# A row of gathers moved beside a projection, eight value buffers, dot products written in place

## The chip, the cores and the metric

The kernel runs on one core of a Trainium2 chip. It uses TensorE (PE in the profile), VectorE (DVE), ScalarE (ACT), GpSimd (POOL) and SyncE (SP), and the core's 16 DMA engines. The metric is the device time of one execution in microseconds, lower is better. The kernel before takes 2611.32 us, the median of three runs (2607.83 to 2613.70).

## The reference, cut to what matters

The reference is two blocks of a network on 256 tokens of width 2048. The first block (attention, a spatial gate, a merge, an output projection) and most of the second are dense products; the change doesn't touch them. It touches the end of the second block, the product-key retrieval of experts, with 8 heads, 16 experts each out of 16384, in two chunks of 128 tokens:

```
def chunk(zc):
    q = (zc @ peer_wq).reshape(128, 8, 2, 128)
    s1 = einsum('chd,hkd->chk', q[:, :, 0], k1);  s2 = einsum('chd,hkd->chk', q[:, :, 1], k2)
    v1, i1 = top_k(s1, 16);  v2, i2 = top_k(s2, 16)
    cand = v1[..., :, None] + v2[..., None, :]          # 16 x 16 sums
    top_s, top_pos = top_k(cand, 16)                    # and the expert numbers i1 * 128 + i2
    gate = softmax(top_s)
    act = gelu(einsum('chkd,cd->chk', peer_u[expert], zc))
    return einsum('chk,chkd->cd', gate * act, peer_v[expert])
```

`peer_u` and `peer_v` have 16384 rows of 2048 float32. Every token takes its own 128 experts, so 2 x 256 x 128 rows of 8 KB are read. The result is added to the residual, and a last RMS norm with the gain `norm_f_g` gives the output.

## The kernel before, in words

All products take their weights in panels of 256 output columns. SP loads a panel as two halves of 1 MB into four slots of RAW; ACT copies each quarter of it rounded into WH; DVE writes the remainder into WL (`split_next`, DVE L1017); PE multiplies WH and WL with the activations' two parts XH and XL (96 matmuls a panel, L1621). PE signals `w_used` after each quarter, and only then may ACT and DVE write the quarter of the next panel. PSUM banks 0 and 1 take the panels in turn, and DVE clears them (`bank_free`). WH, WL, XH and XL lie in the region EX.

The query projection is the last section of that kind: "wq", 8 panels, one per head. DVE clears each panel into `qp` (L1508, in RZ), PE makes the head's key scores for both halves of the tokens (`key_scores`, L1908) after the product of the next panel, and ACT clears these into `scores`. PE also turns the residual into token order with an identity matmul (`token_order`, L1893), 32 instructions for each half; ACT and DVE make of it `znat`, the normed tokens, in two halves (`token_norm`).

A "row" is one head of one half of the tokens: 16 rows, r = 0 to 15, with 16 experts k = 0 to 15. `choose` (DVE) finds the experts of a row in 28 short dependent instructions, in 11 pieces; it leaves their numbers in `idxu` and a copy in `idxv`. In the panels' time `choose` of row 0 lies at panels 1 to 4, that of row 1 at panels 5 to 7.

For each expert k of a row, POOL issues an indirect DMA that gathers 128 rows of `peer_u` (1 MB, one row for each token) into one of four buffers in RAW, and DVE multiplies it with `znat` and sums (the dot, L1542); the products go to two scratch buffers in EX. After 16 dots, DVE and ACT make the row's 16 weights (L1546 to L1557); ACT makes a diagonal matrix of each (L990), and PE multiplies it with the gathered 128 rows of `peer_v` (EX, four buffers, 8 matmul records of L1932) and adds into the half's four PSUM banks. POOL's order is: U gathers of row 0; then for each row r and each k, V gather (r, k) and U gather (r+1, k). Each waits for its buffer to be free. In the last row DVE adds up the experts k with k % 4 in (1, 3) itself (L1578, L1580), and half of the V gathers go to the U buffers. The rows run in hardware loops of two rows for most of the way.

POOL is in order: a gather whose buffer isn't free holds all gathers behind it. The same is true of DVE: a dot whose gather has not landed holds every instruction behind it.

Of the kernel before, what the change touches and what calls it, by code (L numbers as in the profile page):

```python
# [106 lines left out]
def vec_columns():  # L107
# [29 lines left out]
    "dve_step", "act_step", "pool_step", "uz_step", "soft_step", "top_step", "gel_step",  # L137
)
AHEAD = 4


def build(nc, T, out):
# [3 lines left out]
    with ctx:  # L146
# [7 lines left out]
        u_free = [ctx.enter_context(nc.semaphore(f"u_free{s}")) for s in range(4)]  # L154
        v_landed = [ctx.enter_context(nc.semaphore(f"v_landed{s}")) for s in range(4)]
        v_free = [ctx.enter_context(nc.semaphore(f"v_free{s}")) for s in range(4)]
        diag_ready = [ctx.enter_context(nc.semaphore(f"diag_ready{s}")) for s in range(4)]
# [82 lines left out]
        junk = [view(EX, 0, D), view(EX, D, D)]  # L240
        gfbc = view(EX, 2 * D, D)
        vacc = junk[0]
        ON_DVE = (1, 3)

        def last_slot(k):

            s, n = k % 4, k // 8
            if k % 8 < 4:
                return vbuf[s], v_landed[s], (ROWS - 1) * 64 + 16 * (n + 1), v_free[s], (ROWS - 1) * 4 + 1 + n
            return ubuf[s], u_landed[s], ROWS * 64 + 16 * (n + 1), u_free[s], ROWS * 4 + 1 + n  # L250

        ubuf = [view(RAW, (s + 2) % 4 * D, D) for s in range(4)]
        vbuf = [view(EX, (4 + s) * D, D) for s in range(4)]
# [12 lines left out]
        dist = sb("dist", [P, 800])  # L266
        cmask = sb("cmask", [P, 32])
        slopes = sb("slopes", [P, HEADS])
        slcur = sb("slcur", [P, REP])
        gates = sb("gates", [P, HEADS, 6])  # L270

        lruC = gates[:].rearrange("p h s -> p (h s)")[:, 0:8 * BT]
        gcur = sb("gcur", [P, REP, 6])
        vecs = sb("vecs", [P, VEC_COLS])
        hid = sb("hid", [P, 2, 2 * NC_BLOCKS])
        kcT = sb("kcT", [P, 2, NCP])
        kcpad = sb("kcpad", [P, 2, GROUPS, NCP])
        qcur = sb("qcur", [P, 2, TOK])
        vcur = sb("vcur", [P, 5, 3 * HD])
        th = sb("th", [P, 2, PANEL * 2])  # L280
        hidt, hidn = (th[0:SPANS, n, 0:2 * P].rearrange("p (s e) -> p s e", s=2) for n in range(2))
        gin = sb("gin", [P, PANEL * 2])
# [98 lines left out]
        def _(sp):  # L381
# [69 lines left out]
            sp.wait_ge(S["w_used"], QUARTERS * PANELS)  # L451
# [9 lines left out]
        def _(g):  # L461
# [133 lines left out]
            for s in range(4):  # L595
                g.sem_inc(u_free[s], 1)
                g.sem_inc(v_free[s], 1)
# [45 lines left out]
        def _(a):  # L643
# [311 lines left out]
            for j in range(8):  # L955
                if j < 7:
                    split_next("wq", j)
# [1024 lines left out]
```

## Time and profile before

| | |
|---|---|
| median of three runs | 2611.32 us |
| profiled execution | 2612.46 us, its span 2610.7 us |
| PE, busy share | 2204.6 us, 84% |
| DVE | 1523.4 us, 58% |
| POOL | 704.8 us, 27% |
| gathers | 539 MB in 512 gathers |
| DMA rate by fortieths of the span, 1 to 20 | 114 to 261 GB/s |
| 22 to 39 | 403 to 422 GB/s |

The program has two parts. For the first 1300 us PE is busy and the DMA engines are about half busy. From about 1340 us to the end the DMA engines are busy all the time, and PE waits for them. A duration in a row is that of one instruction; behind "idle before" stands for how long the engine did nothing before it, and who ended that. For a POOL gather the duration is that of its issue, not of its transfer.

### The profile page before, as it was taken

How to read it: one execution, taken by the hardware profiler on the slowest of the kernel's cores; microseconds unless marked ns; L12 is line 12 of the kernel's file. 1: busy time of each engine (PE TensorE's matmuls, PEld its weight loads, DVE VectorE, ACT ScalarE, POOL GpSimd, SP SyncE). 2: the span in 40 equal slices, each digit the busy share in tenths (PEclk: the TensorE clock that was granted, in tenths of full speed). 3: DMA queues.
4: the chain of work that ended last, by engine and by line, in shares of the span. 5: the costliest groups of instructions: out<-in, count | busy, mean ns of one | idle time of the engine just before them, and what ended most of it. 6: DMA issues, size and time to landing. Idle time of an engine off the chain costs nothing.

```text
span 2610.7 us, 32711 instructions
## 1 busy us (share of the span) xinstructions
PE 2204.6 (84%) x12156; PEld 1609.4 (62%) x12156; DVE 1523.4 (58%) x2128; ACT 691.4 (26%) x1139; POOL 704.8 (27%) x657
## 2 busy tenths in 40 slices
PE   7999999999999999899937777777777777777776
PEld 7999999999999989899912222222223222332232
DVE  4445655555556587846675565556655556655544
ACT  5434544444344345435300000000000001000001
POOL 3000000000001443020073444434444444444342
PEclk9999999999999999999969999999999999999999
DMA  9634444455657544464499999999999999999997
GB/s 261 193 114 146 138 151 131 137 183 166 222 169 238 162 143 157 135 216 157 146 365 421 421 422 421 421 419 409 403 414 404 422 422 422 418 422 422 421 421 309
DMA packets 280706, 754.64 MB, mean 289 GB/s; under 512 B 11969, under 2 KB 213153, under 8 KB 213793
## 3 DMA queue, kind: packets, MB, share of 16 engines
q0 software_dynamic: 74432, 539.07, 50.3%
q1 hardware_dynamic: 205936, 214.23, 26.2%
q8 instruction: 58, 0.95, 0.2%
q14 instruction: 40, 0.32, 0.0%
q10 hardware_dynamic: 240, 0.07, 0.0%
HBM read 751.22 MB, written 2.10 MB: 289 GB/s over the span
## 4 chain that ended last, share of the span: by engine, by line
PE 55%; DMA 38%; DVE 3%; issue 3%; ACT 1%; POOL 0%; POOLq 0%; DVEq 0%; SPq 0%; ACTq 0%
PE PS L1621 40%; DMA EX<-in_peer_v,idxv 34%; PE PS L1932 9%; DMA RAW<-in_peer_u,idxu 2%; DMA RAW<-in_peer_v,idxv 1%; PE PS L1756 1%; DVE WL L1017 1%; PE PS L1676 1%; PE PS L1734 1%; DVE XL L1027 0%; PE PS L1744 0%; PE PS L1856 0%; POOL RAW L604 0%; PE PS L1758 0%; DMA RZ<-in_x 0%
## 5 line engine op out<-in xcount | busy, mean ns | idle before, releaser
L1932 PE MATMUL PS<-EX,RK 128*128 128x512 f32 x1952 | 914.6, 614 | 355.9 <-DMA EX<-in_peer_v,idxv 273.1
L1932 PEld LDWEIGHTS PS<-EX,RK 128*128 128x128 f32 x1952 | 359.6, 194 | 910.3 <-issue 813.9
L1542 DVE CUSTOM_DVE_ANT_0 EX<-RAW,RZ 128x2048 f32<-128x2048 f32 x256 | 586.8, 2293 | 479.0 <-DMA RAW<-in_peer_u,idxu 435.6
L1621 PE MATMUL PS<-XH,WH 128*128 128x256 f32 x3024 | 839.2, 286 | 11.7 <-DVE WL L1017 8.1
L1621 PE MATMUL PS<-XH,WL 128*128 128x256 f32 x3024 | 832.6, 284 | 0.0
L1621 PE MATMUL PS<-XL,WH 128*128 128x256 f32 x3024 | 761.8, 284 | 5.1 <-DVE XL L1027 3.1
L1017 DVE TENSOR_TENSOR WL<-RAW,WH 128x1024 fp32r<-128x1024 f32 x380 | 480.0, 1274 | 412.1 <-ACT WH L658 409.6
L1621 PEld LDWEIGHTS PS<-XH,WH 128*128 128x128 f32 x3024 | 582.0, 192 | 15.8 <-issue 9.7
L1621 PEld LDWEIGHTS PS<-XH,WL 128*128 128x128 f32 x3024 | 582.2, 193 | 0.0
L658 ACT ACTIVATE WH<-RAW 128x1024 fp32r<-128x1024 f32 x380 | 400.1, 1058 | 566.4 <-PE PS L1621 564.8
L1621 PEld LDWEIGHTS PS<-XL,WH 128*128 128x128 f32 x3024 | 539.9, 193 | 5.9 <-DVE XL L1027 3.5
L604 POOL DMA_INDIRECT EX<-in_peer_v,idxv x240 | 268.5, 1119 | 600.6 <-PE PS L1932 572.8
L604 POOL DMA_INDIRECT RAW<-in_peer_u,idxu x256 | 274.1, 1071 | 201.4 <-DVE WL L1017 90.1
L990 ACT ACTIVATE RK<-identh,wk 128x128 f32<-128x128 f32 x248 | 94.5, 398 | 826.1 <-PE PS L1932 819.5
L518 POOL TENSOR_SCALAR_AFFINE_SELECT RG<-RG 128x1024 f32<-128x1024 f32 x1 | 1.1, 1088 | 514.5 <-ACT RG L791 514.5
L979 ACT ACTIVATE ath<-ain 128x16 f32<-128x16 f32 x16 | 3.5, 216 | 358.4 <-DVE ain L1548 358.4
L524 POOL TENSOR_TENSOR RK<-RZ 128x512 f32 x16 | 17.1, 1068 | 215.6 <-DVE RZ L1283 148.8
L540 POOL MEMSET RK<- 128x1024 f32 x1 | 1.0, 962 | 181.3 <-PE PS L1828 181.3
L768 ACT ACTIVATE RG<-RG,nmx 128x256 f32<-128x256 f32 (+2 forms) x96 | 37.7, 394 | 45.6 <-DVE nmx L1170 45.6
L577 POOL TENSOR_TENSOR RZ<-RZ 128x540 f32<-128x540 f32 (+3 forms) x10 | 15.1, 1508 | 55.3 <-DVE RZ L1315 54.8
L525 POOL TENSOR_TENSOR RK<-RK 128x512 f32<-128x512 f32 x16 | 26.8, 1675 | 1.3
L1174 DVE RECIPROCAL fac<-sums 128x6 f32<-128x6 f32 x16 | 3.1, 192 | 40.3 <-ACT RG L768 40.3
(326 smaller groups left out, 1183.0 us busy)
## 6 DMA issues: line engine op xcount, KB each, us to landing
RAW<-in_w_in SPq DMA_DIRECT2D x110, 1024.0 KB, 5.2
RAW<-in_w_out SPq DMA_DIRECT2D x32, 1024.0 KB, 5.4
RAW<-in_w_ple_gate SPq DMA_DIRECT2D x16, 1024.0 KB, 5.4
RAW<-in_peer_wq SPq DMA_DIRECT2D x16, 1024.0 KB, 5.5
RAW<-in_w_up_a SPq DMA_DIRECT2D x8, 1024.0 KB, 5.4
RAW<-in_w_up_b SPq DMA_DIRECT2D x8, 1024.0 KB, 5.4
RAW<-in_peer_u,idxu POOLq DMA_INDIRECT x256, 16.4
EX<-in_peer_v,idxv POOLq DMA_INDIRECT x248, 15.3
```

What stands on the lines that cost most here:

```text
L525: step(g.tensor_tensor(acc[:, 0], acc[:, 0], sqt[:, 0], ALU.add))
L604: g.indirect_dma_start(buf[s], None, table, bass.IndirectOffsetOnAxis(ap=idx[:, par, k:k + 1], axis=0)).then_inc(landed[s], 16)
L658: a.activation(WH[:, q], raw[:, slot, at:at + QUARTER_KT, :], ACT.Copy).then_inc(S["wh_ready"], 1)
L768: ins = a.activation(eT[:, at:at + size], sT[:, at:at + size], ACT.Exp, bias=nmx[:, n:n + 1], accum_out=sums[:, n:n + 1])
L990: a.activation(diag[:, s, :], identh[:], ACT.Copy, scale=wk[:, par, k:k + 1]).then_inc(diag_ready[s], 1)
L1017: v.tensor_tensor(WL[:, q], raw[:, slot, at:at + QUARTER_KT, :], WH[:, q].bitcast(f32), ALU.subtract).then_inc(S["wl_ready"], 1)
L1542: v.tensor_tensor_reduce(out=junk[k % 2], in0=ubuf[s], in1=znat[:, hf, :], scale=1.0, scalar=0.0, op0=ALU.mult, op1=ALU.add, accum_out=act ...
L1621: ins = mm(o[:, t, :], w[:, q, k, c], x[:, n, :], start=(begins and k == t == m == 0), stop=(ends and k == QUARTER_KT - 1 and m == len(pai ...
L1676: ins = mm(bank(2 + s)[0:SPANS, 0:P], blocks, w1bd[:, s, l, :], start=(l == 0), stop=(l == CMP_LEN - 1))
L1734: mm(pS[:, 0:512], q1, kpad[:, par, :, bass.ds(i, 1), :].rearrange("p t g n -> p (t g) n"), start=True, stop=True)
L1756: mm(pO[:, at:at + size], vcur[:, n, cols], pts[:, src:src + size], start=(par == 0 and n == 0), stop=False, skip_group_check=True)
L1932: ins = mm(bank(4 * hf + c), left, right[:, 512 * c:512 * (c + 1)], start=False, stop=True, skip_group_check=True)
```

## The change

In the panels' time:

- DVE handles `choose` of row 0 in small pieces between the quarters of panels 1 and 2, and then the 16 dots of row 0 between the quarters of panels 3 to 7. `choose` of row 1 comes after the last dot and the weights of row 0.
- The U gathers of row 0 go, one by one, to four places that hold nothing there: two in SM, a new tensor that holds what were small tensors of the attention part, one in the second half of `znat`, one in `qp` (RZ).
- `key_scores` of head j - 1 is put in the middle of product j. `token_order` of the second half of the tokens comes after the last head's scores, and its `token_norm` after row 1. Half 0 of the tokens adds up in banks 4 to 7, and half 1 in banks 0 to 3.

In the rows:

- Dots write their products over their own U buffer, and wait for no dot before them. That makes room for eight V buffers in EX instead of four. POOL issues a V gather when the one eight before it has been used; the V gathers run eight ahead in the order, the U gathers four.
- The load of `norm_f_g` (1 MB) goes to where `norm2_g` lay, after the second `znat`.
- Semaphores that were one for each buffer are now one for each kind, but for those that count landings.

```diff
+V_SLOTS, V_LEAD = 8, 4
-        junk = [view(EX, 0, D), view(EX, D, D)]
-        gfbc = view(EX, 2 * D, D)
-        vacc = junk[0]
+        qlow, qhigh = (view(RZ, 8256 + D * n, D) for n in range(2))
+        def early_ubuf(k):
+            return (SM[:, 0:D], SM[:, D:2 * D], znat[:, 1, :], qhigh if k == 3 else qlow)[k % 4]
+        gfbc = g2bc
+        vacc = qlow
-        vbuf = [view(EX, (4 + s) * D, D) for s in range(4)]
+        vbuf = [view(EX, s * D, D) for s in range(V_SLOTS)]
...
-            sp.wait_ge(S["w_used"], QUARTERS * PANELS)
+            sp.wait_ge(S["znat_ready"], 2)
             sp.dma_start(gfbc, T["norm_f_g_2"].partition_broadcast(P)).then_inc(S["bcf_in"], 16)
...
+            g.wait_ge(S["idx_ready"], 1)
             for k in range(TOPK):
-                if k in (0, 2):
-                    g.wait_ge(S["wl_ready"], QUARTERS * (PANELS - 1 + k // 2))
-                gather_u(0, 0, k)
+                if k >= 4:
+                    g.wait_ge(S["u_used"], k - 3)
+                if k == 7:
+                    g.wait_ge(S["sc_done"], 4)
+                gather(peer_u, early_ubuf(k), u_landed[k % 4], idxu, 0, k)
             g.wait_ge(S["w_used"], QUARTERS * PANELS)
+            for k in range(V_SLOTS):
+                gather_v(0, 0, k, reused=False)
+            for k in range(4):
+                gather_u(1, 1, k, reused=False)
             def gather_row(r, par):
                 for k in range(TOPK):
-                    gather_v(r, par, k)
-                    gather_u(r + 1, 1 - par, k)
+                    if k < 8:
+                        gather_v(r, par, 8 + k)
+                    else:
+                        gather_v(r + 1, 1 - par, k - 8)
+                    if k < 12:
+                        gather_u(r + 1, 1 - par, 4 + k)
+                    else:
+                        gather_u(r + 2, par, k - 12)
...
+            dots = {(3, 4): 1, (4, 1): 2, (4, 2): 3, (4, 3): 4, (5, 1): 5, (5, 3): 6, (5, 4): 7, (6, 1): 8, (6, 2): 9, (6, 4): 11,
+                    (7, 3): 14, (7, 4): 16}
+            for j in range(8):
+                for q in range(QUARTERS + 1):
+                    if j < 7 and q < QUARTERS:
+                        split_next("wq", j, quarters=(q,))
...
+                    for k in range(dotted, dots.get((j, q), dotted)):
+                        dot(0, 0, 0, k, early_ubuf(k))
...
+            def dot(hf, r, par, k, buf):
+                v.wait_ge(u_landed[k % 4], r * 64 + 16 * (k // 4 + 1))
+                v.tensor_tensor_reduce(out=buf, in0=buf, in1=znat[:, hf, :], scale=1.0, scalar=0.0,
+                                       op0=ALU.mult, op1=ALU.add, accum_out=act[:, par, k:k + 1]).then_inc(S["u_used"], 1)
```

DVE at panel 5 of the projection, before. L1508 clears the panel's bank, L1468 to L1448 are the first two pieces of `choose` of row 1, L1017 are the quarters of the next panel.

```order
L1508 TENSOR_TENSOR RZ<-PS,rstd 128x512 [waits w_used]
L1468 COPY RK<-RK 128x256 [waits sc_evac]
L1447 MAX tv<-RK 128x8 [waits top_step]
L1448 MAX_INDEX ti_u<-tv,RK 128x8 [waits top_step]
L1451 MATCH_REPLACE RK<-tv,RK 128x128 [waits top_step]
L1452 MAX tv<-RK 128x8 [waits top_step]
L1453 MAX_INDEX ti_u<-tv,RK 128x8 [waits top_step]
L1447 MAX tv<-RK 128x8 [waits top_step]
L1448 MAX_INDEX ti_u<-tv,RK 128x8 [waits top_step]
L1017 TENSOR_TENSOR WL<-RAW,WH 128x1024 [waits top_step,wh_ready]
L1017 TENSOR_TENSOR WL<-RAW,WH 128x1024 [waits wh_ready] x3
```

The same place now: from the clearing of panel 4 to that of panel 5 and a dot. L1562 clears a bank, L1042 is a quarter, and the two rows of L1526 are one dot.

```order
L1562 TENSOR_TENSOR RZ<-PS,rstd 128x512 [waits u_used,w_used]
L1042 TENSOR_TENSOR WL<-RAW,WH 128x1024 [waits wh_ready] x2
L1526 ISA SM,act<-SM,RZ 128x2048 [waits u_landed0]
L1526 ISA act 128x1
L1042 TENSOR_TENSOR WL<-RAW,WH 128x1024 [waits wh_ready] x2
L1526 ISA SM,act<-SM,RZ 128x2048 [waits u_landed1]
L1526 ISA act 128x1
L1562 TENSOR_TENSOR RZ<-PS,rstd 128x512 [waits w_used]
L1526 ISA RZ,act<-RZ 128x2048 [waits u_landed2]
L1526 ISA act 128x1
```

The short instructions of `choose` have gone from between the quarters, and dots that wait for a landing stand there.

POOL where the panels end, before: the last U gathers of row 0, the start of the loop (it waits for the last panel), and V and U gathers in turn.

```order
L604 DMA RAW<-in_peer_u,idxu 128x2048 [waits u_free2]
L604 DMA RAW<-in_peer_u,idxu 128x2048 [waits u_free3]
L630 UNCONDITIONAL_BRANCH [waits w_used]
L630 ISA
L602 ISA [waits idx_ready]
L604 DMA EX<-in_peer_v,idxv 128x2048 [waits v_free0]
L609 ISA
L602 ISA [waits idx_ready]
L604 DMA RAW<-in_peer_u,idxu 128x2048 [waits u_free0]
```

The same place now: the last four early U gathers, eight V gathers of row 0 behind the last panel, four U gathers of row 1, then V and U in turn.

```order
L604 DMA SM<-in_peer_u,idxu 128x2048 [waits u_used] x2
L604 DMA RZ<-in_peer_u,idxu 128x2048 [waits u_used] x2
L604 DMA EX<-in_peer_v,idxv 128x2048 [waits w_used,idx_ready]
L604 DMA EX<-in_peer_v,idxv 128x2048 x7
L604 DMA RAW<-in_peer_u,idxu 128x2048 [waits idx_ready]
L604 DMA RAW<-in_peer_u,idxu 128x2048 x3
L604 DMA EX<-in_peer_v,idxv 128x2048 [waits v_used]
L604 DMA RAW<-in_peer_u,idxu 128x2048 [waits u_used]
```

Eight V gathers have come ahead of the U gathers of row 1, and only the first of them waits for the panels.

## Rows read from the trace of the kernel before

**Rows 1.** Stretches: busy us of PE, PEld, DVE, ACT, POOL, then PEclk, DMA share, GB/s

```profile
1275.00:1300.00 25.00, 24.31 (x205) 24.04 (x204) 14.45 (x38) 7.37 (x11) 3.23 (x4) 1.00 0.57 212
1300.00:1325.00 25.00, 5.74 (x52) 5.54 (x50) 18.91 (x20) 0.28 (x2) 15.94 (x8) 0.66 0.69 247
...
1725.00:1750.00 25.00, 17.58 (x40) 6.84 (x39) 11.46 (x11) 1.09 (x4) 10.21 (x10) 1.00 1.01 422
```

**Rows 2.** Chain that ended last, 1150 to 1450 us: start, us, what

```profile
1217.68 0.89 PE PS L1908 x8
...
1230.09 3.57 PE PS L1893 x32
...
1284.18 11.53 PE PS L1621 x96
1295.73 0.69 DVE RZ L1508
```

**Rows 3.** DVE in the timeline, dots and row ends: start, us, what, idle before

```profile
1345.57 2.29 DVE L1542 CUSTOM_DVE_ANT_0 EX<-RAW,RZ 128x2048 f32<-128x2048 f32 x1 [0.18 <-DMA RAW<-in_peer_u,idxu]
...
1347.90 0.17 DVE L1546 TENSOR_TENSOR asq<-act 128x16 f32<-128x16 f32 x1
...
2157.79 0.17 DVE L1546 TENSOR_TENSOR asq<-act 128x16 f32<-128x16 f32 x1
...
2237.28 0.17 DVE L1546 TENSOR_TENSOR asq<-act 128x16 f32<-128x16 f32 x1
...
2557.35 0.17 DVE L1546 TENSOR_TENSOR asq<-act 128x16 f32<-128x16 f32 x1
```

**Rows 4.** Costliest groups of the page: count, busy, mean ns, idle before

```profile
L1017 DVE TENSOR_TENSOR WL<-RAW,WH 128x1024 fp32r<-128x1024 f32 x380 | 480.0, 1274 | 412.1 <-ACT WH L658 409.6
```

**Rows 5.** DVE in the three stretches of row 1's choose: length, busy

```profile
1273.80:1277.20 3.40, 2.63 (x13) 1.00 0.29 70
...
1296.30:1301.10 4.80, 3.64 (x13) 1.00 0.62 222
sum 13.10, DVE 10.21; mean DVE 3.40
```

**Rows 6.** POOL in the timeline: the issue of two gathers

```profile
1304.44 2.24 POOL L604 DMA_INDIRECT RAW<-in_peer_u,idxu  x1 [15.68 <-DVE act L1542]
...
1320.94 0.94 POOL L604 DMA_INDIRECT RAW<-in_peer_u,idxu  x1 [0.30 <-issue]
```

**Rows 7.** Transfers from in_peer_u, 1200 to 1400 us, issue to landing

```profile
DMA to landing us min/median/max: 5.6/9.6/16.5
```

**Rows 8.** End of the row at 1752.9 us: DVE, PE and POOL in the timeline

```profile
1759.28 0.29 DVE L1468 COPY RK<-RK 128x256 f32 x1 [5.46 <-issue]
...
1754.47 8.82 PE L1932 MATMUL PS<-EX,RK 128*128 128x512 f32 x16 [2.62 <-ACT RK L990]
...
1760.64 0.94 POOL L604 DMA_INDIRECT EX<-in_peer_v,idxv  x1 [5.74 <-PE PS L1932]
1763.74 0.94 POOL L604 DMA_INDIRECT RAW<-in_peer_u,idxu  x1 [2.16 <-PE PS L1932]
```

**Rows 9.** Last row of experts: DVE and PE in the timeline

```profile
2570.50 2.35 DVE L1580 SCALAR_TENSOR_TENSOR EX<-RAW,wk,EX 128x2048 f32<-128x2048 f32 x1 [2.60 <-DMA RAW<-in_peer_v,idxv]
...
2595.28 2.35 DVE L1580 SCALAR_TENSOR_TENSOR EX<-RAW,wk,EX 128x2048 f32<-128x2048 f32 x1 [2.56 <-DMA RAW<-in_peer_v,idxv]
...
2597.78 3.67 PE L1932 MATMUL PS<-EX,identh 128*128 128x512 f32 x8 [1.22 <-DVE EX L1580]
```

**Rows 10.** DMA issues: KB each, median us from issue to landing

```profile
RAW<-in_peer_u,idxu POOLq DMA_INDIRECT x256, 16.4
...
EX<-in_norm_f_g SPq DMA_DIRECT2D x1, 1024.0 KB, 4.6
```

**Rows 11.** Loads of the projection's panels on SP, and a late quarter on DVE

```profile
1183.68 77.61 SPq L390 DMA_DIRECT2D RAW<-in_peer_wq  x12
...
1281.60 1.23 DVE L1017 TENSOR_TENSOR WL<-RAW,WH 128x1024 fp32r<-128x1024 f32 x1 [1.65 <-ACT WH L658]
```

More of the change, by code:

```diff
@@ L642, in _ @@
+            for k in range(8, TOPK):
+                if k < 12:
+                    g.wait_ge(S["u_used"], ROWS * TOPK + (k - 11))
+                elif k % 4 in ON_DVE:
+                    g.wait_ge(S["v_added"], (k - 12) // 2 + 1)
+                else:
+                    g.wait_ge(S["v_used"], (ROWS - 1) * TOPK + (k - 12) // 2 + 1)
+                buf, landed, _ = last_slot(k)
+                gather(peer_v, buf, landed, idxv, 1, k)
         @block.scalar
@@ L974, in _, with weight_row @@
             expo(0, 1)
-            def weight_row(hf, r, par, last=False):
-                if not last:
+            def weight_row(r, par, first=False, last=False):
+                if not first and not last:
                     expo(1 - par, r + 2)
@@ new lines, in _, with expert_row @@
+            weights(0, 0)
+            v.wait_ge(S["sc_evac"], PEER_HEADS)
+            for piece in range(11):
+                choose(1, 1, CHOOSE, piece)
+            v.tensor_copy(idxu[:, 1, :], expf[:]).then_inc(S["idx_ready"], 1)
+            v.wait_ge(S["idx_ready"], 3)
+            def expert_row(hf, r, par, second=False, last=False):
+                for k in range(TOPK):
+                    if k == V_LEAD:
+                        if not second:
+                            v.wait_ge(S["v_used"], r * TOPK - TOPK)
+                        v.tensor_copy(idxv[:, par, :], idxu[:, par, :]).then_inc(S["idx_ready"], 1)
+                        v.wait_ge(S["idx_ready"], r * 2 + 2)
+                    if k <= 10 and not last:
+                        choose(r + 1, 1 - par, r * CHOOSE + CHOOSE, k)
+                    if k == 11 and not last:
+                        v.tensor_copy(idxu[:, 1 - par, :], expf[:]).then_inc(S["idx_ready"], 1)
+                        v.wait_ge(S["idx_ready"], r * 2 + 3)
+                    dot(hf, r, par, k, ubuf[k % 4])
+                weights(r, par)
@@ L1562, in _ @@
+            expert_row(0, 1, 1, second=True)
+            token_norm(1)
+            v.wait_ge(S["znat_ready"], 2)
             with v.Fori(1, PEER_HEADS // 2) as i:
@@ L1607, in product @@
                 for q in range(QUARTERS):
+                    if q == 2 and middle is not None:
+                        middle()
                     pe.wait_ge(S["wl_ready"], before + (q + 1))
@@ L1912, in _ @@
             for j in range(8):
-                product("wq", j, operand="z3" if j == 0 else None)
+                product("wq", j, operand="z3" if j == 0 else None, middle=(lambda: key_scores(j - 1)) if j else None)
                 if j == 0:
```

273 lines of the change are left out of this document (120 added, 153 removed).

## The prediction

> **What bounds the kernel now.** I read the stretches first. While the projection's panels run, PE is busy nearly all of a stretch and the DMA engines carry 212 GB/s; in the rows of experts the DMA share is 1.01 at 422 GB/s and PE has gaps; between the two lies a stretch with PE busy for 5.7 of 25 us and the DMA at 247 GB/s [rows 1]. So the first part goes by PE, the second by the gathers, and at the seam neither is full. The chain of waits says when the seam begins: the last panel's 96 matmuls run from 1284.18 to 1295.7 us [rows 2]. The timeline of DVE says when it ends: the last dot of row 0 starts at 1345.57, and the row's end (the first instruction of the weights, L1546) is at 1347.90 [rows 3]. Only then can PE use a V gather. Between 1295.7 and 1345.5 the DMA engines have moved 12 U gathers beyond the 4 issued early, for which they need 30 us by the price below; the other 20 us are idle or under-filled.
>
> The price of a gather comes from two row ends with nothing odd between them: 2237.28 - 2157.79 = 79.49 us for 32 gathers [rows 3], 2.484 us each. From 1347.90 to 2557.35 there are 15 rows in 1209.45 us; at 79.49 each they would take 1192.35, so 17.1 us are lost in some rows. One of these shows how [rows 8]: after the row's end DVE stands for 5.46 us before `choose` (wait put down to issue), PE needs 8.82 us for 16 matmul records after a gap of 2.62, and POOL idles 5.74 us before the gather at 1760.64 and 2.16 before the next, while DVE is late with its dots.
>
> **The panels' time.** `token_order` of half 1 leaves it (3.57 us) and one more `key_scores` enters it before the last panel's end (0.89) [rows 2]: PE would end at 1295.73 - 3.57 + 0.89 = 1293.0. DVE gives a quarter's remainder each 2.9 us, at most 1.27 us long [rows 4]. `choose` of row 0 costs 13.1 us, taken as that of row 1 did, in three stretches [rows 5]; with the first `znat` and 8 quarters it fills DVE from about 1218 to 1237.7, when the row's numbers are out. Panel 2 is cleared right behind, at 1238.4, and `key_scores` 2, now in the middle of product 3, would have started at 1236.8: PE waits 1.6 us, which makes 1294.7. The dots follow, each 2.29 us [rows 3]. A panel lasts 4 x 2.88 + 0.89 = 12.4 us, its four quarters and the clearing take 5.4 to 5.8 of DVE, so three dots more make 12.3: it just fits. I laid the order of the new DVE rows against PE's quarters: dots 0 to 3 at 1248.0 to 1262.5, 9 and 10 behind the clearing of panel 6 until 1291.7, 14 and 15 until 1304.5. Panel 7 has no quarters to make behind it, so the five last dots hold only its clearing and the last key scores. The weights come at 1305.9 and `choose` of row 1, in one piece, until 1319.3. The 16 gathers of row 0 need 40 us of DMA between 1238 and 1300, beside the last four or so 1 MB loads; from 57 us to spare that leaves some. PE then turns half 1 until 1305.3 and starts on V at about 1306.5.
>
> **The V gathers** start when the last panel is used, at 1294.7, but POOL still has U gathers 14 and 15 to issue, and a gather that is issued beside a dot takes 2.24 us and not 0.94 [rows 6]. So V 0 goes out at about 1297, V 3 at 1305, V 7 at 1310, and the eighth is down at about 1320.9. U gathers of row 1 can be issued from 1319.6 on, and the first lands no sooner than 5.6 us later [rows 7], at 1325.2; a full stream would have landed it at 1323.4, so 1.8 us are lost.
>
> **The sum.** 512 gathers less 16 of row 0 and 8 V leave 488, of which the first lands at 1325.2 and the last 487 x 2.484 = 1209.7 us later, at 2534.9. The load of `norm_f_g`, 1 MB, lay at 1295.7, where the DMA was idle, and lies in the full stream now: + 2.5 (a gather's price; landing took 4.6 [rows 10]). The losses in rows stay in part. The stand of DVE at the ends of loops stays, since the loops do; U gathers have four buffers as before, so the POOL waits for dots stay. But V gathers waited for PE within each row, and with eight buffers they don't. Before, a V buffer came round in 4 x 4.97 = 19.9 us, of which PE and the issue take 4.5, so that 15.3 us of gathers were queued; with the U buffers as the limit, where the hold is a dot of 2.3, it is 17.3. That is 2 us more cover at each end of a row, and most of the rows lose 1 to 3. I take 6 of 17.1 us as staying; the bounds are 0 and 17.1. It also has the second `znat` (2.35 us of DVE) at the end of row 1. So the last gather lands at 2534.9 + 2.5 + 6 = 2543.4. Before, it landed at 2595.2 (the dot-like sum on DVE starts at 2595.28, released by a DMA), 15.5 us ahead of the span's end; behind it came that sum and the last 8 matmuls [rows 9]. Now the last V gathers are down while PE still has some of its eight to do, which I estimate at 0.7 us: from the last row's weights on PE has eight times 3.67 and the closing sum, beside 12 gathers of 2.484. The span is 2543.4 + 15.5 + 0.7 = 2559.6 us, the execution 1.8 longer than its span as before: **2561 us**. The profiled execution before was 2612.46, 1.1 above its median of 2611.32, so the gain is about 51 us in its own terms, 2%.
>
> What makes it up: 12 gathers out of the full part (30 us), the unfilled rest of the seam (some 13), row losses (11), less 2.5 and less the stretch from 1294.7 to the first V.
>
> The Trainium skill (DMA: Bandwidth & Descriptors, Bandwidth) puts the ceiling at 435.2 GB/s, the SBUF side's 16 ports, and fits the moving part of a DMA as bytes / 436e3 us. By it a gather of 1.049 MB costs 2.41 us, 0.08 less, and with a queue that never runs short the 487 gathers would end 38 us earlier. Against it stands the trace: 422 GB/s at a DMA share of 1.01 [rows 1]. I go by the trace; a deeper queue adds nothing where the share is full.
>
> **Rivals.** *The dots jam the panels.* A dot stands in DVE's queue ahead of quarters that PE needs, so each late landing is PE's wait. If early gathers took the 16.4 us that they take in the full stream [rows 10], four buffers would give four rounds of 16.4 + 2.3 + 1.3 = 20 us: row 0 would be done at 1237.7 + 80 = 1318 and not 1304.5, PE and all behind it 13 us later, 2575 us. Against: four gathers in flight are 10 us of transfer, and 9.6 was the median at the seam [rows 7]. The weight loads are the other side of it. The last of them is issued at about 1261.3, and its quarter is split at 1281.6 [rows 11], 20 us later; a load as slow as a gather would still be in time. The Trainium skill (DMA: Bandwidth & Descriptors, Queues, rings and completion order) says that each DMA engine takes turns between the queues, packet by packet; by it a load would take about twice as long beside gathers, 11 us, inside the 20. 8%.
>
> *The row losses stay whole*, or V buffers were never what mattered: 11 us more, 2572 us. For it: DVE's stand comes first, and the U gather at 1763.74 was issued only after a dot [rows 8]. 8%.
>
> *Slower than before: writing in place makes a dot slow.* It would read and write the same buffer, beside transfers into its neighbours. DVE has 16 dots, 13.1 us of `choose` and about 1.5 of weights a row: 51 us of the gathers' 79.5. From 4.1 us a dot on (28.3 us of room over 16 dots, on top of 2.29) DVE sets the row; the whole gain of 51 us over 15 rows is 3.4 a row, so from 4.3 us a dot on the kernel is slower than before, and at 4.6, twice the time, it takes 15 x 9 us more, some 2690 us with the panels' part. Against: the sums that DVE makes in place today take 2.35 us [rows 9]. 3%.
>
> *No gain to speak of*, several small things together: 1%. My forecast has 80%.
>
> **Range and chances.** With no row loss, no gap and no wait of PE the sum is 2561 - 6 - 1.8 - 1.6 = 2551.6; with all row losses and a panel part 5 us later it is 2577. A little for the lower side: 2549 to 2577, which holds some 85% of the chance. This kernel's runs can't tell less than 0.2% (5 us) from no change. Faster 95%, no change 1%, slower 4%.
>
> **What would show it.** In the changed profile: the last panel's clearing at 1298 to 1300, with PE's last panel done by 1295; early U gathers from 1237 on and 16 dots between 1248 and 1305 of 2.3 us each; the first use of V by PE at 1306 to 1307, where it came behind 1347.90; a first dot of row 1 at about 1325; row ends 79.5 us apart, and fewer that are 81 to 83; POOL's waits put down to dots rather than to PE. Wrong would be PE waiting for L1042 quarters in panels 4 to 7 for more than 5 us together, a dot above 2.5 us, or a DMA rate below 415 GB/s over the rows.

## The result and the profile after

The changed kernel takes 2574.08 us (2573.31 to 2575.16, 4 runs), the kernel before, run beside it on the same chip, 2611.07 us (2607.83 to 2613.7, 4 runs): ratio 0.9859, 95% interval 0.9848 to 0.9871. It is 37 us faster. 2561 us was forecast (some 50 us), within 2549 to 2577. The profiled execution took 2573.31 us with a span of 2571.6.

First the stretches at the seam, in the order of [rows 1], here of the profile after.

```profile
1250.00:1275.00 25.00, 24.81 (x208) 24.61 (x207) 21.54 (x21) 9.31 (x11) 7.16 (x6) 1.00 1.03 386
1275.00:1300.00 25.00, 20.11 (x164) 19.91 (x164) 23.82 (x23) 4.24 (x5) 16.36 (x9) 0.97 0.78 294
1300.00:1325.00 25.00, 24.31 (x80) 13.97 (x78) 15.41 (x52) 5.78 (x14) 13.75 (x12) 0.90 0.99 396
1325.00:1350.00 25.00, 20.65 (x47) 8.30 (x45) 21.25 (x40) 2.27 (x6) 17.86 (x11) 1.00 1.01 422
```

The DMA engines carry 294 and 396 GB/s where they carried 212 and 247 [rows 1], and PE is busy 24.3 us of the third stretch where it was busy 5.7. DVE, in the timeline after: the last panel's clearing, the last dot of row 0, its end, and the first dot of row 1.

```profile
1298.07 0.69 DVE L1562 TENSOR_TENSOR RZ<-PS,rstd 128x512 f32<-128x512 f32 x1
...
1301.58 2.29 DVE L1526 CUSTOM_DVE_ANT_0 RZ<-RZ 128x2048 f32<-128x2048 f32 x1 [0.23 <-DMA RZ<-in_peer_u,idxu]
...
1303.92 0.17 DVE L1532 TENSOR_TENSOR asq<-act 128x16 f32<-128x16 f32 x1
...
1326.02 2.29 DVE L1526 CUSTOM_DVE_ANT_0 RAW<-RAW,RZ 128x2048 f32<-128x2048 f32 x1 [7.10 <-DMA RAW<-in_peer_u,idxu]
```

Row 0 ends at 1303.92 where it ended at 1347.90 [rows 3], 44 us sooner; the dot in place takes 2.29 us as before. POOL and PE at the same place: the first V gathers, the first U gather of row 1, the first use of V.

```profile
1296.07 2.88 POOL L604 DMA_INDIRECT EX<-in_peer_v,idxv  x1 [0.30 <-issue]
...
1304.99 0.94 POOL L604 DMA_INDIRECT EX<-in_peer_v,idxv  x1 [0.30 <-issue]
...
1318.50 0.94 POOL L604 DMA_INDIRECT RAW<-in_peer_u,idxu  x1 [7.60 <-DVE idxu L1582]
```

```profile
1301.58 5.56 PE L1937 MATMUL PS<-ident,RZ 128*128 128x128 f32 x32 [0.69 <-ACT RK L979]
1306.97 3.60 PE L1971 MATMUL PS<-EX,RK 128*128 128x512 f32 x8
```

Up to here the plan was kept to within a microsecond or two. The rows were not. DVE after: the ends of rows 1, 7, 8, 9, 10, 11 and 15, the stands behind rows 9 and 11, and the last sum on DVE.

```profile
1395.75 0.17 DVE L1532 TENSOR_TENSOR asq<-act 128x16 f32<-128x16 f32 x1
...
1876.28 0.18 DVE L1532 TENSOR_TENSOR asq<-act 128x16 f32<-128x16 f32 x1
1956.81 0.17 DVE L1532 TENSOR_TENSOR asq<-act 128x16 f32<-128x16 f32 x1
2038.31 0.17 DVE L1532 TENSOR_TENSOR asq<-act 128x16 f32<-128x16 f32 x1
2044.77 0.29 DVE L1493 COPY RK<-RK 128x256 f32 x1 [5.52 <-issue]
2120.59 0.17 DVE L1532 TENSOR_TENSOR asq<-act 128x16 f32<-128x16 f32 x1
2202.31 0.17 DVE L1532 TENSOR_TENSOR asq<-act 128x16 f32<-128x16 f32 x1
2208.71 0.29 DVE L1493 COPY RK<-RK 128x256 f32 x1 [5.45 <-issue]
...
2527.04 0.18 DVE L1532 TENSOR_TENSOR asq<-act 128x16 f32<-128x16 f32 x1
...
2554.68 2.35 DVE L1620 SCALAR_TENSOR_TENSOR RZ<-EX,wk,RZ 128x2048 f32<-128x2048 f32 x1 [2.57 <-DMA EX<-in_peer_v,idxv]
```

The 14 rows from 1395.75 to 2527.04 take 1131.29 us; at 79.49 [rows 3] they would take 1112.9. So 18.4 us are still lost, 2.5 of them the load that was priced apart. Row by row, with ends read as above, in us:

| rows | 2 | 3 | 4 | 5 | 6 | 7 | 8 | 9 | 10 | 11 | 12 | 13 | 14 | 15 |
|---|---|---|---|---|---|---|---|---|---|---|---|---|---|---|
| before | 80.1 | 81.5 | 82.4 | 81.4 | 82.6 | 81.9 | 80.5 | 80.4 | 79.5 | 79.5 | 79.5 | 79.5 | 80.5 | 80.5 |
| after | 82.1 | 80.3 | 79.6 | 79.5 | 79.5 | 79.5 | 80.5 | 81.5 | 82.3 | 81.7 | 82.4 | 81.7 | 80.1 | 80.5 |

The slow rows have not gone. They have moved, from rows 3 to 7 to rows 9 to 13, and the stands with them (a stand: DVE idle for 5.5 us behind a row's end, with no wait that the profile shows), from the ends of rows 3 and 5 ([rows 8] shows the second) to those of rows 9 and 11. Nothing in the change was meant to move them. In sum the rows cost what they cost before: rows 2 to 15 took 1129.9 us before and 1131.3 now, so none of the 37 us lies there. POOL's waits in the rows are put down to DVE and to PE by turns, the latter up to 7.4 us (POOL after, 1400 to 2520 us: us in total, times, longest):

```profile
POOL RAW L604 <- DVE act L1526: 377.0, 135, 3.7
POOL EX L604 <- PE PS L1971: 91.8, 18, 7.4
```

### The profile page after: what moved, and what is told of

Its sections match the earlier page's. It is cut to its first block, busy times and chain, and to the rows that moved or that the text cites. A ratio compares the mean times of both kernels' runs of the same rounds, so it can differ in the third digit from the quotient of the medians.

```text
span 2571.6 us, 32853 instructions
## 1 busy us (share of the span) xinstructions
PE 2166.3 (84%) x12092; PEld 1627.0 (63%) x12092; DVE 1520.6 (59%) x2128; ACT 694.0 (27%) x1141; POOL 717.5 (28%) x657
## 4 chain that ended last, share of the span: by engine, by line
PE 53%; DMA 31%; DVE 6%; issue 6%; POOL 1%; ACT 1%; POOLq 0%; DVEq 0%; ACTq 0%; SPq 0%
PE PS L1663 39%; DMA RAW<-in_peer_u,idxu 30%; PE PS L1971 9%; DVE WL L1042 1%; DVE RAW L1526 1%; PE PS L1798 1%; POOL EX L604 1%; PE PS L1718 1%; POOL RAW L604 1%; PE PS L1776 1%; DMA EX<-in_peer_v,idxv 0%; DVE XL L1052 0%; PE PS L1786 0%; PE PS L1898 0%; DVE RZ L1526 0%
## 5 line engine op out<-in xcount | busy, mean ns | idle before, releaser
L1971 PE MATMUL PS<-EX,RK 128*128 128x512 f32 x1968 | 888.9, 613 | 356.4 <-ACT RK L1012 338.7
L1971 PEld LDWEIGHTS PS<-EX,RK 128*128 128x128 f32 x1968 | 384.5, 197 | 859.9 <-issue 803.2
L1663 PE MATMUL PS<-XH,WH 128*128 128x256 f32 x3024 | 840.2, 286 | 10.5 <-DVE WL L1042 6.9
L1526 DVE CUSTOM_DVE_ANT_0 RAW<-RAW,RZ 128x2048 f32<-128x2048 f32 x240 | 550.2, 2292 | 467.9 <-DMA RAW<-in_peer_u,idxu 465.0
L1042 DVE TENSOR_TENSOR WL<-RAW,WH 128x1024 fp32r<-128x1024 f32 x380 | 480.2, 1275 | 398.4 <-ACT WH L685 395.8
L685 ACT ACTIVATE WH<-RAW 128x1024 fp32r<-128x1024 f32 x380 | 400.2, 1058 | 566.7 <-PE PS L1663 566.7
L604 POOL DMA_INDIRECT RAW<-in_peer_u,idxu x240 | 252.2, 1051 | 510.5 <-DVE act L1526 401.0
L604 POOL DMA_INDIRECT EX<-in_peer_v,idxv x252 | 288.7, 1146 | 180.8 <-PE PS L1971 97.7
L531 POOL TENSOR_TENSOR RK<-RZ 128x512 f32 x16 | 17.1, 1067 | 215.5 <-DVE RZ L1308 148.8
L604 POOL DMA_INDIRECT SM<-in_peer_u,idxu x8 | 12.6, 1580 | 70.3 <-issue 44.8
```

The lines of the kernel that those rows point to most:

```text
L604: g.indirect_dma_start(buf, None, table, bass.IndirectOffsetOnAxis(ap=idx[:, par, k:k + 1], axis=0)).then_inc(landed, 16)
L685: a.activation(WH[:, q], raw[:, slot, at:at + QUARTER_KT, :], ACT.Copy).then_inc(S["wh_ready"], 1)
L1042: v.tensor_tensor(WL[:, q], raw[:, slot, at:at + QUARTER_KT, :], WH[:, q].bitcast(f32), ALU.subtract).then_inc(S["wl_ready"], 1)
L1526: v.tensor_tensor_reduce(out=buf, in0=buf, in1=znat[:, hf, :], scale=1.0, scalar=0.0, op0=ALU.mult, op1=ALU.add, accum_out=act[:, par, k:k ...
L1663: ins = mm(o[:, t, :], w[:, q, k, c], x[:, n, :], start=(begins and k == t == m == 0), stop=(ends and k == QUARTER_KT - 1 and m == len(pai ...
L1971: ins = mm(bank(4 * (1 - hf) + c), left, right[:, 512 * c:512 * (c + 1)], start=False, stop=True, skip_group_check=True)
```

## The experiments

Each was timed beside the kernel before. The groups ran on different chips, where the kernel before took 2608.9 to 2611.1 us, so differences of some 2 us between groups say nothing. Two theories stood at the start: V gathers held by buffers that PE has not used yet (A), and DVE's stands (B).

**V four places ahead.** The order of V gathers in POOL's program, nothing else:

```
-                    if k < 8:
-                        gather_v(r, par, 8 + k)
...
+                    elif 4 + k < TOPK:
+                        gather_v(r, par, 4 + k)
                     else:
-                        gather_v(r + 1, 1 - par, k - 8)
+                        gather_v(r + 1, 1 - par, 4 + k - TOPK)
...
```

> The changed kernel with one thing altered: the order in which V gathers stand among the U gathers. Eight V buffers stay, but V runs four places ahead of the row, not eight, so that gather 8 of a row stands 8.5 pairs (42 us) behind the row's last U gather, not 4.5 (22 us). Theory A (the losses of the rows, 15.9 us over 14 rows plus 2.5 for a load, come from V gathers whose buffer PE has not yet used at the row's start): POOL's waits for PE at row starts go, rows take 79.5 us nearly everywhere, and the time falls by 10 to 16 us, to 2558 to 2564 us. Theory B (they come from DVE standing 5.5 us at loop ends, and late dots holding the four U buffers): same rows as in the changed kernel, within 3 us of 2574 us.

2572.23 us (2572.02 to 2572.86), ratio 0.9853, interval 0.9838 to 0.9868: 2 us at most. POOL waited for PE ahead of V gathers twice where it had waited 18 times, and the rows still took 1132.2 us:

```profile
POOL RAW L604 <- DVE act L1531: 543.7, 192, 3.8
...
POOL EX L604 <- PE PS L1976: 6.6, 2, 3.9
```

The waits went and the time stayed: theory A fell. Of 5 us stretches here, those from the stand at 2195 us on have the lowest DMA rate:

```profile
2195.00:2200.00 5.00, 4.26 (x6) 1.84 (x7) 0.09 (x1) 1.28 (x4) 1.76 (x2) 0.66 1.01 418
2200.00:2205.00 5.00, 4.57 (x11) 1.71 (x9) 3.82 (x9) 0.80 (x2) 0.00 (x0) 1.00 0.87 359
2205.00:2210.00 5.00, 3.67 (x8) 1.44 (x8) 4.11 (x8) 0.01 (x1) 4.38 (x3) 1.00 0.74 242
2210.00:2215.00 5.00, 2.79 (x5) 1.35 (x6) 2.52 (x8) 0.40 (x1) 4.10 (x3) 0.84 0.95 329
```

DVE is busy 0.09 us of the first one; POOL issues nothing in the second; the rate falls to 242 GB/s in the third. I took that for the loss. The trace's landing times say otherwise: from 2190 to 2225 us the gathers land 2.46 to 2.73 us apart, dip or not, but for three spacings of 3.44 to 3.46 us, whose cause comes below.

**DVE's loops written out.**

```
-            with v.Fori(1, PEER_HEADS // 2) as i:
-                for par in range(2):
-                    expert_row(0, i * 2 + par, par)
-            with v.Fori(PEER_HEADS // 2, PEER_HEADS - 1) as i:
-                for par in range(2):
-                    expert_row(1, i * 2 + par, par)
+            for r in range(2, ROWS - 2):
+                expert_row(r // PEER_HEADS, r, r % 2)
```

> The changed kernel with DVE's two loops over the rows of experts written out, and nothing else. Theory B (DVE's stands of 5.5 us at loop ends, some 12.8 us in eight places, make the rows' losses): they go and the time falls by 8 to 13 us, to 2561 to 2566 us. Theory A (V buffers decide at the row's start): the stands may go, the row losses stay, 2571 to 2576 us. A third possibility: written out, the instructions come from memory anyway and DVE stands more often, which would show as stands elsewhere and a time up to 10 us longer.

2567.89 us (2564.78 to 2568.98), ratio 0.9837, interval 0.9824 to 0.9851: 6 us faster than the changed kernel where theory B said 8 to 13, and no stand is left. But now 8 of rows 2 to 15 took 80.4 to 80.5 us, where the best are 79.5. This is what led further.

**Four V buffers; and products apart.** The first has four V buffers and the order of before; the second also writes the products of rows 1 to 15 to two buffers apart (`out=junk[k % 2]`, with a wait for the dot two back), so that of the change only the early row is left.

```
-V_SLOTS, V_LEAD = 8, 4
+V_SLOTS, V_LEAD = 4, 4
...
```

> The changed kernel with four V buffers and the order of V and U gathers that the kernel before had; the early first row and the dots in place stay. It is the changed kernel without its deeper V buffers. Theory A (eight buffers spent on a longer lead give no slack): within 3 us of 2574 us. The prediction's step (deeper V buffers take away 11 us of row losses): 11 us longer than with eight, 2585 us; if part of it was right, in between.

> As the one with four V buffers, and the dots of rows 1 to 15 also write their products to two buffers apart, as in the kernel before; of the change only the early first row stays. Both theories: a dot is 2.29 us in place or not, so the same time as with four V buffers, within 2 us, and the whole gain of 37 us is that of the early row. If writing in place costs or gives something, it shows as a dot other than 2.29 us and a time apart by 15 x 16 x the difference where DVE is late.

Four buffers: 2580.27 us (2579.84 to 2580.95), ratio 0.9884, interval 0.9869 to 0.9899. Products apart too: 2581.61 us (2580.59 to 2584.55), 0.9892, interval 0.9877 to 0.9907. So the early row alone is worth 28 us of the 37, the eight buffers 6 (the prediction's step had asked for 11), and the dots in place nothing that can be told (2293 ns a dot in place, 2292 apart). The place of the loops doesn't blur this: with products apart rows 2 to 15 took 1131.9 us, as long as in the changed kernel. The 6 us of the buffers are not in the rows: row 15 ends at 2526.40 with four and at 2527.04 with eight. They are behind it. With four:

```profile
2520.00:2525.00 5.00, 3.71 (x10) 1.44 (x8) 2.40 (x3) 0.00 (x0) 1.02 (x1) 1.00 0.76 259
2525.00:2530.00 5.00, 2.61 (x7) 1.06 (x6) 2.98 (x8) 1.50 (x5) 2.87 (x4) 1.00 0.66 238
```

and with eight, the changed kernel:

```profile
2520.00:2525.00 5.00, 0.00 (x0) 0.00 (x0) 2.31 (x3) 0.00 (x0) 0.00 (x0) 0.50 1.01 421
2525.00:2530.00 5.00, 1.53 (x2) 0.84 (x3) 4.79 (x9) 1.50 (x5) 4.46 (x2) 0.50 1.02 423
```

In the last row no U gathers are left, and here V gathers filled the stream with eight buffers and not with four.

**Both fixes at once, the dot first, and the late load.** Four kernels: V four ahead with the loops written out; the changed kernel with each dot ahead of the piece of `choose`; all three; and with it `sp.wait_ge(S["v_added"], TOPK // 2 - 1)` ahead of the load of `norm_f_g` in place of `sp.wait_ge(S["znat_ready"], 2)`.

```
-                    if k <= 10 and not last:
-                        choose(r + 1, 1 - par, r * CHOOSE + CHOOSE, k)
...
                     dot(hf, r, par, k, ubuf[k % 4])
+                    if k <= 10 and not last:
+                        choose(r + 1, 1 - par, r * CHOOSE + CHOOSE, k)
```

> V four places ahead and DVE's loops written out, both at once. One alone gave 2572.2 us, the other 2567.9 us. With V four ahead the DMA dips that stayed (2200 to 2215 us, 359, 242 and 329 GB/s) stood at DVE's stand of 5.5 us; written out with V eight ahead the dips that stayed (one a row, 310 to 400 GB/s) stood at POOL's wait for PE. Theory C (two holders of POOL's queue at each row's start, DVE's late dots and PE's late use of V, each of which covers the other): together they give more than the sum of 2 and 6 us, about 12 us, 2560 to 2563 us, and rows of 79.5 us. Theory D (the two are independent): 2566 us. Theory E (a row's start costs about 1 us whatever is done, since dots stand behind the choice of the next row's experts): rows of 80.5 us stay, 2568 us.

> The changed kernel with, in each place of a row on DVE, the dot ahead of the piece of the choice for the next row and not behind it; nothing else. The first dot of a row, whose gather is long down, starts about 2.5 us sooner, and with it POOL's next U gather. Theory C (late dots hold POOL's queue at the row's start, PE's late use of V does too): DVE's part shrinks by 2.5 us at each start that has a stand, PE's stays; 2 to 5 us faster, 2569 to 2572 us. Theory A (only PE's use of V): no change, 2573 to 2575 us.

> All three: V four ahead, DVE's loops written out, the dot ahead of the choice. Theory C: no holder is left at a row's start, every row is 79.5 us, and the time is 2558 to 2561 us. Theory E: with the dot first its 1 us a row goes too, 2556 to 2560 us. If the time is that of the one without the dot first, within 2 us, DVE's order was covered already.

> As the last, and the load of norm_f_g (1 MB) goes behind the seventh of the last row's eight sums on DVE, where the DMA queues run dry, and not into the full stream. The prediction priced it at a gather's place there, 2.5 us: 2.5 us faster than without it if it lands by the last division by the norm, which starts some 5 us after that sum; if it comes too late for it, up to 2 us of that are lost again.

| kernel | us | runs | ratio, interval |
|---|---|---|---|
| V four ahead, written out | 2568.31 | 2564.14 to 2569.39 | 0.9839, 0.9826 to 0.9853 |
| dot first | 2572.52 | 2570.76 to 2573.32 | 0.9854, 0.9839 to 0.9869 |
| all three | 2567.06 | 2565.55 to 2568.44 | 0.9835, 0.9821 to 0.9848 |
| and the late load | 2565.37 | 2564.49 to 2565.65 | 0.9828, 0.9814 to 0.9841 |

The late load gives 1.7 us where 2.5 were expected, and the intervals overlap: it can't be told from nothing. Theory C fell: nothing adds to the written-out loops. Rows of 80.5 us stay with every holder gone, with the dot first too, so the reason that theory E gave falls as well. In these rows the DMA is never low (411 to 428 GB/s in each 5 us from 1960 to 2180 us), and most dots come 4.97 us apart. But with all three there are eight gaps of 5.8 to 6.0 us, behind the dots at 1718, 1809, 1899, 1995, 2090, 2195, 2286 and 2381 us. Beside each, within 3 us, one packet is listed for a queue of instructions (q14), and there are none of them between 1614 and 1720. The changed kernel shows the same. DVE's dots at 2179 us, and the queues from 2181 to 2185 us:

```profile
2174.17 2.29 DVE L1526 CUSTOM_DVE_ANT_0 RAW<-RAW,RZ 128x2048 f32<-128x2048 f32 x1 [2.06 <-DMA RAW<-in_peer_u,idxu]
2179.26 2.29 DVE L1526 CUSTOM_DVE_ANT_0 RAW<-RAW,RZ 128x2048 f32<-128x2048 f32 x1 [2.69 <-DMA RAW<-in_peer_u,idxu]
2185.07 2.29 DVE L1526 CUSTOM_DVE_ANT_0 RAW<-RAW,RZ 128x2048 f32<-128x2048 f32 x1 [3.51 <-DMA RAW<-in_peer_u,idxu]
```

```profile
q0 software_dynamic: 236, 1.67, 101.1%
q14 instruction: 1, 0.01, 0.5%
```

The dot at 2185 us waited for a landing, so DVE was not what was late. Nor was POOL: that gather was issued at 2167.30, 3.72 us behind the one ahead of it as in the pairs around it, and took 17.74 us to land where the last U gather had taken 16.78.

The queue brought 0.32 MB in 39 packets over the whole of the changed kernel, 8 KB each. With all three edits the trace lists 1034 DVE instructions, waits and branches included, between the packets at 1613 and 2383 us, in eight spacings: 129 to a packet, 63 bytes each. The Trainium skill (Runtime: NRT & Kernel Launch, Instruction fetch mechanics) gives 256 instructions to 16 KiB, 64 bytes each; the trace agrees on the bytes of an instruction, while its packets are of 8 KB. So q14 most likely carries DVE's code, and the runs below, which alter DVE's program alone, move its packets.

The slow rows are those in which code comes. Over rows 4 to 13 of all fourteen traces (before, after and the twelve runs), by the number of these packets in a row:

| packets of q14 in the row | rows | their lengths, us |
|---|---|---|
| 0 | 56 | 79.4 to 79.7 |
| 1 | 49 | 80.0 to 80.6 |
| 2 | 19 | 81.4 to 82.0 |
| 3, each row with a stand | 12 | 82.3 to 82.9 |
| 4, each row with a stand | 4 | 83.4 |

About 1 us for each packet, and a stand adds nothing to that. The landings show it gather by gather: in these rows they come 2.4 to 2.8 us apart, except beside a packet of q14, where nearly all spacings are 3.4 to 3.5 us, and each packet has its long spacing (I leave out the run with everything together, whose trace lacks some landings). The rows at either end follow less well: row 15 of the changed kernel had three packets and took 80.5 us.

**Moving the loops.** A stand was now read as DVE fetching the head of its loop again, and the place of the loop in the code as what decides. Counted in the built program, the loops before begin at instruction 1036 and 1340 (302 long), after at 1007 and 1287 (278 long). (These counts are short, as the padded kernel before shows below.)

```
+            for _ in range(32):
+                v.wait_ge(S["znat_ready"], 2)
+                v.nop(nofuse=True)
             with v.Fori(PEER_HEADS // 2, PEER_HEADS - 1) as i:
```

Each wait and its `nop` are one instruction of the built program. The counter-test has 24 such waits ahead of the first loop, `with v.Fori(1, PEER_HEADS // 2) as i:`, and none ahead of the second.

> The changed kernel with 32 waits on DVE between its two loops over rows, on a semaphore that is long there; nothing else. DVE's first loop is instructions 1007 to 1284 of its program, the second 1287 to 1564; the second now begins at 1319. Over before, after and the one with products apart, loops that begin at 7, 12 or 254 modulo 256 have the stands of 5.5 us at their back-edges, loops that begin at 54, 60 or 239 have none. Theory F (DVE holds two blocks of 256 instructions, with a boundary between 12 and 29 modulo 256; a body that touches three blocks has to be brought again at each back-edge, and each 8 KB of instructions that come make a gather land 1 us later): at 39 the second loop touches two blocks, both stands go, so do the instruction packets in rows 8 to 13, these rows go from 80.5 to 82.4 us to 79.5, and the time falls by 8 to 13 us, to 2561 to 2566 us, below the written-out loops (2567.9), since those bring all their instructions. Theory A (the rows' losses come from V buffers): 2574 us, or 1 more for the waits.

> The counter-test: 24 such waits on DVE ahead of its first loop over rows. By theory F the first loop (from 1031, 7 modulo 256, to 29) now touches three blocks and the second (from 1311, 31 modulo 256) two. So the stands of 5.5 us leave the back-edges at the ends of rows 9 and 11 and appear at the ends of rows 3 and 5, rows 2 to 7 go from 79.5 to about 81.5 us and rows 8 to 13 to 79.5, and the time stays near the changed kernel's: 2572 to 2577 us. If the stands hung on what the loop does and not on where its code lies, they would stay in the second loop.

Ahead of the second: 2562.68 us (2561.28 to 2565.28), ratio 0.9824, interval 0.9811 to 0.9838, 11 us faster than the changed kernel by the medians, 9 by the ratios, for 32 instructions that do nothing. Both stands are gone. Rows 10 to 13 took 79.5, 79.6, 79.5 and 79.5 us; rows 8 and 9, which were to fall to 79.5 too, took 81.5 and 80.5, with two packets and one, as DVE comes to new code there. Over rows 2 to 15 it is 10 packets for 20, and 1120.9 us for 1131.3. Queues from 2100 to 2380 us, first of the changed kernel, then of this one:

```profile
q0 software_dynamic: 15744, 114.68, 99.5%
q14 instruction: 7, 0.06, 0.1%
```

```profile
q0 software_dynamic: 16211, 118.09, 101.3%
```

No code comes, and 3.41 MB more of gathers are carried in the same time, 8 us' worth at 421 GB/s. Ahead of the first: 2572.22 us (2569.37 to 2573.37), 0.9857, interval 0.9842 to 0.9872, with DVE's stands as foretold at the ends of rows 3 and 5 (this kernel, DVE in the timeline):

```profile
1566.43 0.30 DVE L1493 COPY RK<-RK 128x256 f32 x1 [6.53 <-issue]
...
1730.18 0.29 DVE L1493 COPY RK<-RK 128x256 f32 x1 [6.47 <-issue]
...
2049.71 0.47 DVE L1493 COPY RK<-RK 128x256 f32 x1 [0.37 <-issue]
```

Its rows 4 and 6 took 83.4 us, rows 10 to 13 79.5. The same instructions stand or don't, by where they lie: theory F held at both, but for rows 8 and 9 of the first.

**The same on the kernel before, and everything together.** 20 waits ahead of the first loop of the kernel before; and the changed kernel with the 32 waits, V four ahead, the dot first and the late load.

```
+            for _ in range(20):
+                v.wait_ge(S["znat_ready"], 2)
+                v.nop(nofuse=True)
             with v.Fori(1, PEER_HEADS // 2) as i:
```

> The kernel before, with 20 waits on a semaphore that is long there ahead of DVE's first loop over rows; nothing else. Its first loop began at 1036 (12 modulo 256) and had the stands, its second at 1340 (60) had none; now they begin at 1056 (32) and 1360 (80), and by theory F both touch two blocks. Its rows 3 to 7 took 81.4 to 82.6 us and should take 79.5: 10 us or so less, 2597 to 2602 us. So the 17.1 us that the prediction saw lost in the rows of the kernel before would be this for the greater part, and none of it the V buffers. If the losses were V gathers waiting for PE, 2607 to 2612 us.

> The changed kernel with the 32 waits ahead of DVE's second loop (2562.7 us alone), V four places ahead (-1.9 alone), the dot ahead of the choice (-1.6 alone) and the late load of norm_f_g (-1.7 beside the written-out loops). If all add, 2557.5 us; if those three only covered what the stands held, 2561 to 2563 us.

The kernel before with 20 waits: 2610.79 us, ratio 1.0006, interval 0.9997 to 1.0015. A miss. The stands had not moved:

```profile
1593.47 0.29 DVE L1468 COPY RK<-RK 128x256 f32 x1 [5.50 <-issue]
...
1757.71 0.29 DVE L1468 COPY RK<-RK 128x256 f32 x1 [5.76 <-issue]
```

Its rows 4 and 6 took 83.4 us with four packets each, its rows 10 to 13 79.4 to 79.5 with none: the price of a packet held, the placement missed.

What failed is the count. From one back-edge to the next the trace lists 296 DVE instructions where the built program of the changed kernel has 278, and 320 where that of the kernel before has 302: each MAX_INDEX and MATCH_REPLACE of the program is two instructions in the trace. Counted so, the loops begin at:

| kernel, loop | start | modulo 256 | length | stands |
|---|---|---|---|---|
| changed, first | 1034 | 10 | 296 | no |
| products apart, first | 1049 | 25 | 328 | yes |
| 24 waits, first | 1058 | 34 | 296 | yes |
| before, first | 1063 | 39 | 320 | yes |
| changed, second | 1332 | 52 | 296 | yes |
| before with 20 waits, first | 1083 | 59 | 320 | yes |
| 24 waits, second | 1356 | 76 | 296 | no |
| 32 waits, second | 1364 | 84 | 296 | no |
| products apart, second | 1379 | 99 | 328 | no |
| before, second | 1385 | 105 | 320 | no |
| before with 20 waits, second | 1405 | 125 | 320 | no |

With a block boundary anywhere from 60 to 73 modulo 256, the bodies that stand touch three blocks of 256 and the others two, in all eleven; with the built program's counts no boundary does that. So the rule of two blocks fits every run, and the padded kernel before ended short of the boundary. This is one number fitted afterwards, and no run was forecast from it: 34 waits would clear the boundary in the kernel before wherever it lies in that range, and were not tried. Three blocks of 128 fit as well. One thing speaks for a fixed boundary on its own: behind the second loop the first packet came with DVE at instruction 1734 to 1742 by this count, 70 to 78 modulo 128, in all six kernels of the table, though their programs differ.

All together: 2560.57 us (2557.74 to 2562.45), ratio 0.9812, interval 0.9798 to 0.9825, the fastest here, 1.9% under the kernel before and 0.5% under the changed one. If all had added it would have been 2557.5. The three small edits that it has beyond the 32 waits can't be told from nothing: the interval overlaps that of the waits alone.

## Why the prediction was right, and where it was wrong

The direction was right, and so were the place of most of the gain, the seam, and its mechanism. The step on the rows was wrong: the time that came is, within 2 us, that of the rival "the row losses stay whole", and the range held it because it reached up to 2577. In the profiled span 2571.6 was measured for 2559.6, 12.0 us more. By its own steps:

- *The panels' time.* PE was to lose 1.6 us and finish at 1294.7; its last matmul of a panel began at 1293.6, the clearing came at 1298.07 (1298 to 1300 foretold), the weights at 1303.92 (1305.9), `choose` of row 1 was done at 1317.6 (1319.3). 1 to 2 us better. The dots did not jam the panels: from 1240 to 1300 us PE waited 5.1 us for DVE's clearings, 4.9 of them behind the last panel.
- *The V gathers.* V 0 at 1296.07 (1297), V 3 at 1304.99 (1305), V 7 at 1309.96 (1310). PE's first use of V at 1306.97 (1306.5). The first dot of row 1 at 1326.02 (1325.2): +0.8 us. POOL's issues of 2.2 to 2.9 us beside dots were as read in [rows 6].
- *The dots in place* cost nothing: 2.29 us; the rival that would have made the kernel slower fell with it.
- *The price of a gather* held wherever no code came (79.5 us a row). For the load of `norm_f_g` 2.5 us were foretold. Row 2, in which it lies, took 82.1 us, but 81.2 and 81.5 in the two kernels that load it later, and it has two packets of code in all three: the load's own price isn't shown.
- *The row losses* are the step that failed: "most of the rows lose 1 to 3. I take 6 of 17.1 us as staying", because V gathers would no longer wait for PE. From 1326.02 to the last landing at 2554.68 are 1228.7 us; 487 x 2.484 + 2.5 = 1212.2; so 16.5 stayed: +10.5 us, nearly the whole miss. The cause of the loss was misread. Of the two candidates in [rows 8], DVE's stand behind the row's end and POOL's wait for PE, I took the second for what deeper buffers cure, and left the first as a constant. The deeper buffers did what they were to do: POOL's idle time put down to PE ahead of V gathers fell from 572.8 to 97.7 us, as the signs foretold, and the rows were not shorter. V four ahead took nearly all of the rest away, and they kept their length again. The 32 waits took ten packets of code away, and about 10 us went from the rows. The other sign, fewer rows of 81 to 83 us, didn't come: five before, six now. The rival, 2572 us at 8%, had been told that way, and I had its reason nearly in words: "DVE's stand comes first". But the stand is the sign of the loss and not its price; the price is 1 us for each packet of code. In rows 4 to 13 before, 12 packets and 12 us over 79.5 a row make up the greater part of the 17.1. The trace of before had the clue, which I passed over by adding 15 rows into one sum: its rows 10 to 13 took 79.5 us, its rows 4 and 6 82.4 and 82.6, with the same code in them. A held buffer would have cost alike in both loops.
- *The end.* From the last landing to the span's end 16.9 us, foretold 16.2: +0.7. The 6 us that eight buffers are worth lie behind the end of row 15. The sum had them without naming them, as it let the stream run full to the last gather.

0.8 + 10.5 + 0.7 = 12.0 us. The Trainium skill (Runtime: NRT & Kernel Launch, Instruction fetch mechanics) says that an engine's instruction memory is two blocks of 256 instructions, filled in sequence, and that a branch out of the two waits for a fetch. With the trace's counts the eleven placements above agree. The page also calls the crossing of a block mostly hidden, and names the stall at a branch as one reason why kernels prefer full unrolling. Here a crossing wasn't hidden: each packet of code in a full DMA stream made one gather about 1 us late. The loop which stays in place took 2562.7 us and the one written out 2567.9 us; the ratios' intervals overlap (0.9811 to 0.9838, 0.9824 to 0.9851), but rows 2 to 15 have 10 packets and 15, and took 1120.9 and 1125.3 us.

What stays open: why a packet of 8 KB costs a gather 1 us. By the share shown above (0.5% of 16 engines over 4 us) it took 0.3 us of one engine's time. Nor do the bytes explain it: another queue of instructions, q8, brings packets of 16 KB, and beside those at 2043 and 2076 us in the kernel with 32 waits the landings stayed 2.5 us apart.

## What to carry to other kernels

Where alike rows of a loop differ in length, list them side by side, by loop, before giving the excess to a buffer: an excess that one loop has and its twin with the same code lacks points at the code's place. In a kernel that the DMA bounds, count the packets of the queues of instructions in each row, and look at the spacing of landings and not at the DMA rate, whose dips here cost next to nothing. A few idle instructions ahead of a loop gave 9 to 11 us here, the four added V buffers 6. And a change that alters the length of an engine's code moves its loops, so that 10 us of a measured gain or loss can come from that alone: compare the packets before crediting the edit. To place a loop, count the instructions that the trace lists and not those of the program.

## What the runs showed that I had not expected

- With V eight ahead PE has nothing to do for 22.5 us at the end of the row shown here, and starts the next at the granted clock of 0.5 (1.2 GHz). From 2115 to 2120 us PE is busy 0.00 us at a granted clock of 0.50, from 2120 to 2125 it starts at 0.50, and from 2130 it has 1.00. PE in the timeline of the changed kernel:

```profile
2122.18 28.37 PE L1971 MATMUL PS<-EX,RK 128*128 128x512 f32 x59 [22.47 <-ACT RK L1012]
```

The mean granted clock fell from 0.98 to 0.926 over the span and rose to 0.982 with V four ahead; the time moved by 2 us, since PE doesn't bound the rows.
- The dot ahead of `choose` changed nothing that can be told (2572.52 for 2574.08 us). It was expected to start a row's first dot 2.5 us sooner. The first dot came 2.6 us behind the end of row 5 for 2.9, and 6.5 for 7.9 behind that of row 9, where the stand is; POOL's first V gather behind that end came after 9.0 us in both. A gather takes 16.4 us from issue to landing in the full stream [rows 10], and that much queued work can hide small delays of POOL.
